# Latent attention: where the five filler matmuls of an item stand

## The reference

```python
def attend_block(args):
    qn_b, qr_b, start = args
    s = (einsum('bqhd,bkhd->bhqk', qn_b, k_nope)
         + einsum('bqhd,bkd->bhqk', qr_b, k_rope)) * scale
    causal = k_pos[None, :] <= q_pos[:, None]
    s = where(causal, s, -inf)
    p = softmax(s, axis=-1).astype(v.dtype)
    return einsum('bhqk,bkhd->bqhd', p, v)
```

## Time and profile before

| | |
|---|---|
| median of 3 runs | 2129.03 us (2127.67 to 2131.23) |
| the profiled execution | 2131.52 us |
| its span on the core | 2129.7 us |
| mean granted clock | 0.99 |
| TensorE busy | 2062.0 us (97%) |
| ScalarE, VectorE, GpSimd busy | 35%, 38%, 37% |

### The profile page before, as it was taken

The page is one execution under the profiler, slowest core; times in us unless marked ns, Lnnn a source line. Parts: engine busy times, 40 slices in busy tenths (PEclk is TensorE's granted clock), DMA queues, the critical chain, the costliest instruction groups (busy, mean ns, idle before and its releaser), DMA issues.

```text
span 2129.7 us, 32015 instructions
## 1 busy us (share of the span) xinstructions
PE 2062.0 (97%) x13924; PEld 1768.5 (83%) x13924; DVE 815.4 (38%) x1284; ACT 736.3 (35%) x1139; POOL 778.8 (37%) x246
## 2 busy tenths in 40 slices
PE   7999999999999999999999989999999999999998
PEld 6899888878977789999999867798777788888886
DVE  3400675145357655220222241256566544211222
ACT  5423222336556544221222353342222333212222
POOL 4443332545322154334433421035244235334432
PEclk9999999999999999999999999999999999999999
DMA  5223122222210122223322430031113133223322
GB/s 172 90 89 112 52 75 79 79 89 80 94 59 28 40 79 80 80 75 106 98 72 88 101 99 30 31 96 60 42 61 111 62 98 99 87 77 114 99 65 74
DMA packets 170036, 171.52 MB, mean 81 GB/s; under 512 B 16924, under 2 KB 160664, under 8 KB 169896
## 3 DMA queue, kind: packets, MB, share of 16 engines
q1 hardware_dynamic: 168492, 167.25, 24.9%
q10 hardware_dynamic: 1404, 2.23, 0.3%
HBM read 163.17 MB, written 6.29 MB: 80 GB/s over the span
## 4 chain that ended last, share of the span: by engine, by line
PE 88%; DVE 5%; issue 3%; ACT 2%; POOL 1%; DMA 1%; ACTq 0%; SPq 0%; DVEq 0%; POOLq 0%
PE ps L2080 86%; PE ps L2082 2%; DVE coef L1575 1%; POOL w_lo L752 1%; ACT w_hi L891 0%; ACT diag L919 0%; DMA x_rows<-in_x 0%; DVE gdn_x L1945 0%; DVE u_lo L1392 0%; POOL stat L769 0%; DVE tmp L1404 0%; DVE neg_max L1563 0%; DVE gdn_inv_t L1928 0%; ACT u_hi L945 0%; DVE mla_q L1748 0%
## 5 line engine op out<-in xcount | busy, mean ns | idle before, releaser
L752 POOL TENSOR_TENSOR w_lo<-w_raw,w_hi 128x2048 fp32r<-128x2048 f32 (+3 forms) x157 | 674.6, 4299 | 942.2 <-ACT w_hi L891 936.7
L2080 PE MATMUL ps<-u_hi,w_hi 128*128 128x512 f32 (+1 forms) x1904 | 585.6, 347 | 19.1 <-POOL w_lo L752 5.7
L2080 PE MATMUL ps<-u_hi,w_lo 128*128 128x512 f32 (+1 forms) x1904 | 580.4, 345 | 0.0
L2080 PE MATMUL ps<-u_lo,w_hi 128*128 128x512 f32 (+1 forms) x1904 | 571.0, 345 | 1.1 <-DVE u_lo L1392 0.8
L2080 PEld LDWEIGHTS ps<-u_hi,w_hi 128*128 128x128 f32 x1904 | 329.7, 189 | 62.8 <-issue 10.4
L2080 PEld LDWEIGHTS ps<-u_lo,w_hi 128*128 128x128 f32 x1904 | 327.2, 189 | 44.1 <-DVE u_lo L1392 5.5
L2080 PEld LDWEIGHTS ps<-u_hi,w_lo 128*128 128x128 f32 x1904 | 329.2, 189 | 40.3 <-issue 0.5
L891 ACT ACTIVATE w_hi<-w_raw 128x2048 fp32r<-128x2048 f32 (+3 forms) x157 | 279.9, 1784 | 178.2 <-PE ps L2080 168.9
L2080 PE MATMUL ps<-hidden_hi,w_hi 128*128 128x264 f32 (+1 forms) x528 | 141.1, 321 | 0.0
L2080 PE MATMUL ps<-hidden_lo,w_hi 128*128 128x264 f32 (+1 forms) x528 | 141.0, 322 | 0.0
L2080 PE MATMUL ps<-hidden_hi,w_lo 128*128 128x264 f32 (+1 forms) x528 | 140.8, 321 | 0.0
(11 more groups left out here) (376 smaller groups left out, 2948.0 us busy)
## 6 DMA issues: line engine op xcount, KB each, us to landing
w_raw<-in_w_in_a SPq DMA_DIRECT2D x23, 1024.0 KB, 5.2
w_raw<-in_ffn_w_gate SPq DMA_DIRECT2D x22, 1024.0 KB, 5.3
w_raw<-in_ffn_w_up SPq DMA_DIRECT2D x22, 1024.0 KB, 5.3
w_raw<-in_w_in SPq DMA_DIRECT2D x17, 1024.0 KB, 5.4
w_raw<-in_ffn_w_down SPq DMA_DIRECT2D x16, 768.0 KB, 4.4
w_raw<-in_ffn_w_down SPq DMA_DIRECT2D x16, 640.0 KB, 4.2
w_raw<-in_w_out_a SPq DMA_DIRECT2D x8, 1024.0 KB, 5.2
w_raw<-in_w_kv SPq DMA_DIRECT2D x8, 1024.0 KB, 5.4
```

The lines of the kernel that those rows point to most:

```text
L752: pool.tensor_tensor(WL[:, u % RAWS, part], RAW[:, u % RAWS, part], WH[:, u % SPLITS, part].bitcast(F32), ALU.subtract).then_inc(lo_done, 1)
L2080: return nc.tensor.matmul(o, a, b, start=start, stop=stop, **kw)
```

## The change

The two counts of the table change from 2 and 3 to 5 and 0: all fillers of a step stand behind its causal mask, none behind its transposes. Nothing else is edited; what the table feeds (VectorE's and ScalarE's steps) follows.

```diff
-            for site, n in (("scored", 2), ("turned", 3)):
+            for site, n in (("scored", 5), ("turned", 0)):
```

## The result

The changed kernel took 2137.24 us in the median of 22 runs, the kernel before 2129.47 us in 22 runs beside it. The ratio is 1.0028, with a 95% interval of 1.0016 to 1.0039: 3.4 to 8.3 us slower (it agrees with the ratio of the means, 2136.09 to 2130.21; the two medians alone would give 1.0036). Twelve further runs gave 2135.34 us and 1.0020 (1.0006 to 1.0034). One further execution of the kernel before, beside the last experiments, took 5114.74 us and is left out everywhere. The forecast of 2132.5 us had too little (+3.6 us for a measured +6.0); the range held the time, and the side was the first rival's, not the forecast's own case.

The account below looks back on a forecast made before the run. TensorE, busy 97% of the span, was taken to bound the kernel. Boundaries 1.2, last items 1.1, plain items 0 and clock 1.3 summed to +3.6 us on a 2129.03 median, say 2132.5 us; range 2128.0 to 2138.5.

Parts of the forecast that it names:

- first rival: Clock falls at every boundary, items 5, 10, 15, 20, 25: +9.8 us, 2138.8 us; decides from the fourth fall; chance 0.34.
- forecast's own case: Five longer gaps, earlier filler end and three short clock falls give +3.6 us, just within 0.2%; chance 0.47.
- The order that results: Item loop: every filler chunk ends behind a mask; boundaries at items 5, 10, 15, 20, 25; fillers end in item 29.
- Part 1, the boundaries: TensorE idle at five chunk boundaries while VectorE reads the bank: 6.62 us against 5.46 before, +1.16 us.
- Part 2, the last items: Items 30 and 31 lose their fillers, so item 31's value products wait uncovered: +1.1 us, bounds 0 to 1.4.
- Part 3, the plain items: Other items: same fillers and products, transposes 0.7 us later with room for it: 0, bounds 2.6 us either way.
- Part 4, the clock: TensorE's clock falls behind gaps: 5.1 us after against 4.6 before, plus 0.8 at the loop's end, together +1.3 us.
- the short kind: Clock fall behind a boundary gap, priced at 1.7 us because five fillers in a row follow; taken three times in five.
- What I said would prove me wrong: Median moving by more than 4.3 us with no more than three falls, or TensorE waiting for ScalarE in plain items.

Follow-up runs that it names:

- the kernel with the late end: Changed kernel with two of the six chunks giving four fillers per item, so fillers end in item 31 instead of 29: 2137.40 us, 1.0025.
- the kernel before with busy gaps: Kernel before, with one or two extra products of about 0.5 us in each of its five gaps: 2126.64 us, 0.9986.
- The experiment with the old order in plain items: Changed kernel, but items that don't begin a chunk have two fillers behind the mask, three behind the transposes: 2138.34 us, 1.0035.
- turned boundaries: Changed kernel with fillers behind the transposes in the five items that begin a chunk: 2128.90 us, 0.9993; with fillers also ending in item 31: 2126.38 us, 0.9982.

## Why the prediction was right or wrong

*The order that results* was right in each point: five restarts, all directly behind the mask, no fillers from item 30 on.

*Part 1, the boundaries:* forecast 6.62 us of gaps, measured 6.7; three single gaps 1.34, 1.36, 1.49 forecast and 1.35, 1.36, 1.49 measured. The other two missed and nearly made up for each other, which was luck: item 20 has 1.31 for a forecast 1.09, item 25 has 1.22 for 1.34. At item 20 VectorE began the gate row 0.43 us behind the start of the row maximum; in the kernel with the late end, at item 16 of the same width, it was 0.22, and the gap 1.09. Why VectorE's two instructions lie closer in one item than in the other stays open.

*Part 2, the last items:* an idle time of 1.10 us stands before item 31's value products, as worked out. Item 0 to 31 is 2.9 us longer without falls (109.06 against 106.14), and from item 31 to the next stage, at the full clock, it is 0.3 shorter: 1397.79 - 1388.88 = 8.91 against 1385.29 - 1376.10 = 9.19 in the kernel before with busy gaps. (The 9.84 of before's own profile, 1390.60 - 1380.76, hold 2.4 us at the lower clock.) The next stage's first product in the two, after and before with busy gaps:

```profile
1397.79 0.51 PE L2080 MATMUL ps<-u_hi,w_hi 128*128 128x264 f32 x2
```

```profile
1385.29 0.51 PE L2080 MATMUL ps<-u_hi,w_hi 128*128 128x264 f32 x2
```

Together 2.6 for parts 1 and 2, or 2.4 by the estimate over all runs, against a forecast of 2.3.

*Part 3, the plain items:* nothing, as forecast. The experiment with the old order in plain items has the whole loss, and the one with the new order in them has none.

*Part 4, the clock,* was mis-sized, and it is the term that decided. It was put at +1.3 us: two falls in the median execution before (4.6 us), three short ones after (5.1), and 0.8 at the loop's end. The runs say 3.0 to 4.7 for the changed kernel's boundary falls alone (from 1.0028 and 1.0020 to 1.0006 when the gaps are busy), and before's own falls cost 3 us (0.9986 when busy). The four profiles with the changed kernel's five sites, bare gaps and early end (three of its own, one with plain items as before) have 10.2, 10.2, 20.5 and 20.5 us at the lower clock between items 0 and 31, the two of before 13.7 and 3.4: on average 7.7 against 4.3 us of price, +3.4; the estimate over all runs has +3.1. With the fixed 2.4 to 2.6 that is 5.5 to 6.0, where the two measured ratios say 6.0 and 4.3.

The term that was mis-sized is the price of a fall after the change. For before, two falls and 4.6 us were taken, and its two profiles have two on average and 4.3 us. For after, three falls were taken, and the four profiles have 13 in 20 gaps, 3.25 each: the count was nearly right. But each was priced at 1.7 us, "the short kind", because five fillers in a row follow the gap. All 13 have five fillers behind them, and they cost 2.4 us each: ten lasted 3.4 us, two 6.8 and one 13.7. Of the 2.6 us that 5.1 lacks to 7.7, the price makes 2.1 and the count 0.4. The 0.8 for the loop's end did not show either: in its three profiles the clock fell 7.7 to 9.6 us behind the start of item 31's row maximum, before in its two 7.4 and 7.5. The first rival started at the fourth fall and got 0.34; the changed kernel's three profiles have two, three and five falls, so neither the case nor the rival is the typical execution, and the time lies between them. That the range held 2137.24 us rests on its width as much as on the sum.

*What I said would prove me wrong* (a median more than 4.3 us off with no more than three falls) came true with the first profile (two falls) and with the third (three), not with the second (five). It was a fair warning: the number of falls could not carry the loss at the price taken for one. But a count in one profile is a poor test of a term that varies from one execution to the next. The other sign, a wait of TensorE for ScalarE in plain items, did not come.

*The Trainium skill* ("TensorE: Matmul & The Clock Gate", section "Why this matters for your kernels") would have allowed all these gaps, being far under 3 us. The runs differ: in each of the five profiles with five bare gaps behind a mask, gaps of 1.09 to 1.49 us, the clock fell once to five times, and at none of the gaps when TensorE worked through them. The Trainium skill says in "What's actually happening", on the same page, that the chip's watch over activity runs freely and isn't tied to the kernel. That agrees with what the profiles show: items 15 and 20 in one execution, items 5, 10 and 25 in another, all five in a third.

## What to carry to other kernels

A wait of one to one and a half microseconds on a busy TensorE can cost as much by the clock as by its length: here five such gaps, 6.5 us of waiting, cost 6.0 us more when they were empty than when TensorE worked through them (1.0025 against 0.9997). Two things helped in these runs: work that nobody needs in the gap, and the transposes that were ready anyway moved into it, which also shortened it (6.7 to 4.6 us in all). When fillers are moved, look first at the few places where the queue really waits: the count per item decided nothing here, five items of 30 decided everything. And when the terms at stake are falls of the clock, take several profiles and time in many runs before one profile is explained.

## What the runs showed that I had not expected

A gap of 1.09 to 1.49 us directly behind a mask brought the clock down 14 times in 25 (five profiles of five gaps: three of the changed kernel, one with plain items as before, one with the late end), the shortest of these gaps among them; before's two gaps of this kind (1.49 and 1.36) did so in one of its two profiles. With transposes ahead of them the gaps were 0.2 to 1.2 us; none of ten brought it down in the two profiles with turned boundaries, but before's longest of that kind, 1.16 us at item 27, did so in both of its profiles, and four gaps of 1.14 and 1.16 us in the turned kernels did not. So whether the transposes protect a gap or only shorten it is not shown. With extra products in the gaps there was no fall in 20 gaps of four profiles. Directly behind a mask it took two products, about 1.0 us, in each gap; whether one would do was not tried there. And the kernel before had more to give than its share of busy time (97%) suggests: turned boundaries in all five places and fillers to the last item take 0.18% off it, without a product more.
